# Strassen weight sums made in place, a weight ring of five, and a regrouped ConvFFN tail in a streaming encoder

## The reference

```python
h = rms_norm(x, norm1_g)
z = h @ w_in                       # 1024 x 4608: A value, A gate, B's B, C and v, merge gates
u = a_val * sigmoid(a_gate)
u = silu(layer_norm(causal_dwconv31(u) + b_dw_a))
y_a = u @ w_a_out
y_b = (b_g * causal_dwconv3(c_g * b_val)) @ w_b_out
x = x + (sigmoid(gA) * y_a + sigmoid(gB) * y_b) @ w_o
f_gate, f_val = split(rms_norm(x, norm2_g) @ w_up)       # 2 x 2816
x = x + (silu(causal_dwconv3(f_gate)) * f_val) @ w_down
y = rms_norm(x, final_g)
```

## Time and profile before

| | |
|---|---|
| Median of 3 runs | 1561.84 us (1561.3 to 1563.38) |
| Profiled execution | 1564.04 us, of which span 1561.1 us |
| PE, DVE, ACT, POOL busy | 90%, 71%, 34%, 5% of the span |
| Mean granted clock of PE | 0.969 of full |
| HBM read | 87.77 MB |

### The profile page before, as it was taken

One profiled execution on the slowest core, in us unless ns is written; L12 is line 12 of the kernel. 1 busy time (PEld: TensorE's weight loads), 2 busy tenths in 40 slices (PEclk: granted clock), 3 DMA queues, 4 the chain that ended last, 5 costly groups with the idle time before them and its releaser, 6 DMA issues.

```text
span 1561.1 us, 25790 instructions
## 1 busy us (share of the span) xinstructions
PE 1403.1 (90%) x10658; PEld 1369.0 (88%) x10658; DVE 1111.0 (71%) x1622; ACT 525.4 (34%) x854; POOL 79.5 (5%) x88
## 2 busy tenths in 40 slices
PE   4799999899996899997989999999999999999967
PEld 2699999898986899986889898999999898989967
DVE  5989999998865443467776667676667766676745
ACT  6743322333433333345422222323222222223122
POOL 2000000000000042211000000000000000000001
PEclk9999999999998899988899999999999999999988
DMA  5121111122214353321111111111121111111013
GB/s 167 49 74 48 48 55 48 63 83 98 99 65 147 112 180 106 89 61 48 55 47 42 48 35 55 41 42 55 31 64 35 48 41 48 35 55 35 27 41 116
DMA packets 137659, 102.98 MB, mean 66 GB/s; under 512 B 5389, under 2 KB 130055, under 8 KB 137543
## 3 DMA queue, kind: packets, MB, share of 16 engines
q1 hardware_dynamic: 134716, 92.21, 19.5%
q10 hardware_dynamic: 2827, 9.13, 1.5%
HBM read 87.77 MB, written 13.55 MB: 65 GB/s over the span
## 4 chain that ended last, share of the span: by engine, by line
PE 46%; DVE 28%; issue 10%; ACT 8%; DMA 6%; POOL 1%; ACTq 0%; SPq 0%; DVEq 0%
DVE cv L1297 6%; PE BA L369 5%; PE BC L369 5%; PE BA L371 5%; PE BA L370 5%; PE BC L371 5%; PE BC L370 5%; DMA w_raw<-in_w_down 4%; DVE cvf L1532 4%; DVE w_lo L1115 4%; ACT w_hi L749 3%; PE BB L369 3%; PE BB L370 3%; PE BB L371 3%; PE BS L369 2%
## 5 line engine op out<-in xcount | busy, mean ns | idle before, releaser
L1115 DVE TENSOR_TENSOR w_lo<-stg,w_hi 128x512 fp32r<-128x512 f32 x301 | 214.4, 714 | 130.5 <-ACT w_hi L749 129.6
L749 ACT ACTIVATE w_hi<-stg 128x512 fp32r<-128x512 f32 x301 | 187.9, 626 | 292.2 <-PE BA L371 91.3
L369 PE MATMUL BB<-hb,w_hi 128*128 128x272 f32 x788 | 233.1, 296 | 35.1 <-ACT ss_f L831 22.6
L369 PE MATMUL BA<-hb,w_hi 128*128 128x272 f32 x812 | 238.7, 294 | 23.9 <-DVE t_out L1195 8.1
L370 PE MATMUL BA<-hb,w_hi 128*128 128x272 f32 x812 | 235.7, 290 | 0.0
L371 PE MATMUL BA<-hb,w_lo 128*128 128x272 f32 x812 | 235.6, 290 | 0.0
L370 PE MATMUL BB<-hb,w_hi 128*128 128x272 f32 x788 | 229.7, 291 | 0.0
L371 PE MATMUL BB<-hb,w_lo 128*128 128x272 f32 x788 | 229.2, 291 | 0.0
L369 PE MATMUL BC<-hb,w_hi 128*128 128x272 f32 x640 | 187.3, 293 | 14.6 <-ACT ss_f L822 12.4
L1115 DVE TENSOR_TENSOR w_lo<-w_raw,w_hi 128x512 fp32r<-128x512 f32 x92 | 68.2, 741 | 167.6 <-ACT w_hi L749 167.0
L369 PEld LDWEIGHTS BB<-hb,w_hi 128*128 128x128 f32 x788 | 151.6, 192 | 40.7 <-ACT ss_f L831 25.0
(11 more groups left out here) (285 smaller groups left out, 3136.0 us busy)
## 6 DMA issues: line engine op xcount, KB each, us to landing
stg<-in_w_up SPq DMA_DIRECT2D x92, 256.0 KB, 3.0
stg<-in_w_in SPq DMA_DIRECT2D x80, 256.0 KB, 2.9
w_raw<-in_w_down SPq DMA_DIRECT2D x44, 256.0 KB, 2.7
gate_spill<-t_out ACTq DMA_DIRECT2D x16, 544.0 KB, 3.2
gates<-gate_spill SPq DMA_DIRECT2D x16, 544.0 KB, 4.5
w_raw<-in_w_o SPq DMA_DIRECT2D x32, 256.0 KB, 2.9
xr<-in_x_prompt SPq DMA_DIRECT2D x8, 512.0 KB, 5.8
out_y_prompt<-out_rows SPq DMA_DIRECT2D x8, 512.0 KB
```

Of the source, the lines that this page charges most:

```text
L369: pe.matmul(dst, w_hi[:, w, at:at + P], hi, start=first, stop=False, skip_group_check=True)
L749: act.activation(w_hi[:, n % RING, :], src, ACT.Copy).then_inc(whi, 1)
L1115: dve.tensor_tensor(out, full, high.bitcast(F32), ALU.subtract).then_inc(done, 1)
```

## The change

It has eight parts.

1. RING = 5 and LOOK = 4. `stg` shrinks from eight buffers to four.
2. The four sums are made in the place of their first terms: SP loads A22, A11, A12 and A21 into `stg[S1]`, `stg[S2]`, `stg[S4]`, `stg[S3]` (`first_terms`), and DVE adds in place (`weight_sums`), as a first step of `lo(n)` where product n + 1 has a sum as its weight. With LOOK = 4 that is in slots 3 (one sum), 4 (two) and 5 (one).
3. A11, A12 and A22 as weights of products 0, 5 and 6 are loaded a second time, by `plain_weights`, into the ring. A job has seven loads instead of four.
4. ConvFFN's `ss5` has two buffers, used by turns.
5. The groups of the last two pairs are ordered as job 41, job 42, `down(9)`, `down(10)`; the operands of f = 20 and 21 get places of their own (`qt_hi`, `qt_lo`, `qt_raw`).
6. `qb` is split in jobs 18 and 19 (blocks 0 and 1) and after job 19 (2 and 3). The adds for `e_b` move from POOL to DVE, slot 0 of job 19. The first mean part moves from behind product 1 to behind product 2, its copies to slots 4 and 6.
7. `ln_part` moves from h = 6, 7 to h = 7, 8, and both row copies stand in m = 4. In ConvFFN's first job `ms_columns(1)`, `root_diagonal(1)`, `rb_part(1)` and `rb_copy(1)` move back, the last two into the next job.
8. At the start, the rows of the second half of the tokens are normalised, turned and split later (`evac` in slots 4 to 11), job 0's sums are spread over its `lo` calls, and the fourth row tile is loaded ahead of the weights.

The table TAPS is the same in both kernels.

```diff
-RING = 4
-LOOK = 3
+RING = 5
+LOOK = 4
...
-    N_WD.append(BASE[-1] + 7)
+    BASE += [BASE[-1] + 7, BASE[-1] + 14]
+    N_WD += [BASE[-1] + 7, BASE[-1] + 11]
...
-    stg = place("stg", [P, 8, 4 * P], F32)
+    stg = place("stg", [P, 4, 4 * P], F32)
...
-    ss5_f = place("ss5_f", [P, 2, HP], F32, SS_AT + 8 * HP)
+    ss5_f = [place(f"ss5_f{s}", [P, 2, HP], F32, SS_AT + 8 * HP * (1 + s)) for s in range(2)]
...
-                    elif h in (6, 7):
-                        ln_part(h - 6)
+                    elif h in (7, 8):
+                        ln_part(h - 7)
...
-            job(J_F, [None, None, lambda: ms_columns(1), None, None, lambda: rb_part(1)])
-            job(J_F + 1)
+            job(J_F, [None, None, None, lambda: ms_columns(1)])
+            job(J_F + 1, [None, lambda: rb_part(1)])
...
+            job(f_job(KF - 2))
+            job(f_job(KF - 1))
+            down(G - 2)
...
+                    elif j > J_F + 2:
+                        act.wait_ge(n2, N2[j - 2])
                     act.activation(ss5(j), BC[:, ps, 0:HP], ACT.Copy).then_inc(cp, 1)
...
+            def qb_split_hi(k):
+                act.wait_ge(x_dve, X_DVE[J_S - 1])
+                if k == 1:
+                    act.wait_ge(wlo, BASE[J_F - 1] + 5)
+                elif k == 2:
+                    act.wait_ge(used, N_P1)
+                act.activation(qb_hi[k][:, :], bv[:, k, :], ACT.Copy).then_inc(qb_hid, 1)
...
+            def weight_sums(j, s):
+
+                terms = {S1: ((S1, S3),), S2: ((S3, S2), (S2, S1)), S4: ((S4, S2),), S3: ()}[s]
+                for a, b in terms:
+                    dve.wait_ge(base_in[a], 16 * (j + 1))
+                    dve.wait_ge(base_in[b], 16 * (j + 1))
+                    if a != S1:
+                        dve.wait_ge(wsum, 4 * j + SUM_NO[a] - 1)
+                    dve.tensor_tensor(stg[:, a, :], stg[:, a, :], stg[:, b, :], ALU.add).then_inc(wsum, 1)
+
             def lo(n):
+
+                if n + 1 in SUMMED:
+                    weight_sums(*SUMMED[n + 1])
...
+                    if j == J_F - 1 and s == 0:
+                        dve.wait_ge(tap_done, KA * TAPS_A)
+                        dve.tensor_tensor(e_b[:, :], cv[0][:, :], cv[1][:, :], ALU.add).then_inc(e_sum, 1)
...
+            def first_terms(j):
 
                 src = w_in_cols if j < J_F else w_up_cols
                 c1, c2 = job_cols(j)
+                for s, t, c, last in ((S1, 1, c2, 3), (S2, 0, c1, 4), (S4, 1, c1, 4), (S3, 0, c2, 5)):
+                    if j == J_F:
+                        sp.wait_ge(used, N_P2)
+                    elif j:
+                        sp.wait_ge(wlo, BASE[j - 1] + last)
+                    sp.dma_start(stg[:, s, :].rearrange("p (k c) -> p k c", k=KJ),
+                                 src[:, :, t, c:c + P]).then_inc(base_in[s], 16)
+
+            def job_weights(j):
...
                 if j:
+                    plain_weights(BASE[j], src[:, :, 0, c1:c1 + P])
+                if j + 1 < len(JOBS) and j + 1 != J_F:
+                    first_terms(j + 1)
+                plain_weights(BASE[j] + 5, src[:, :, 1, c1:c1 + P])
+                plain_weights(BASE[j] + 6, src[:, :, 1, c2:c2 + P])
```

More of the change, by code:

```diff
@@ L123, in streaming_encoder @@
     UP = at[0]
-    A11, A12, A21, S2, S3, S4, A22 = 0, 1, 2, 3, 4, 5, 6
-    S1 = A21
+    S1, S2, S4, S3 = range(4)
     T1N, T3, T2N, T4, B11, B21, B22 = range(7)
@@ L551, in _ @@
                             a = PW * p + HP * c
[L552 removed]
+                            last = three(bank[:, c, 0:HP], n % RING, k * P, qb_hi[k][:, a:a + HP], qb_lo[:, k, a:a + HP],
                                          k == 0, k == KB - 1)
@@ L634, in _ @@
             G = KF // 2
-            for i in range(1, G):
+            for i in range(1, G - 1):
                 job(f_job(2 * i))
@@ L733, in hi @@
                     act.wait_ge(used, n - RING + 1)
-                if n in DIRECT:
-                    act.wait_ge(w_in[n % RING], DIRECT[n])
+                if n in PLAIN:
+                    act.wait_ge(w_in[n % RING], PLAIN[n])
                     src = w_raw[:, n % RING, :]
                 else:
[L738 to L748, removed]
+                    j, s = SUMMED[n]
+                    act.wait_ge(wsum, 4 * j + SUM_NO[s])
+                    src = stg[:, s, :]
                 act.activation(w_hi[:, n % RING, :], src, ACT.Copy).then_inc(whi, 1)
@@ L952, in row_copy @@
                 act.activation(sq_a[:, lo:up], flat(BB)[:, 0:up - lo], ACT.Copy).then_inc(row_out, 1)
-            act.wait_ge(used, N_P1)
-            act.wait_ge(x_dve, X_DVE[J_S - 1])
-            for k in range(KB):
-                act.activation(qb_hi[:, k, :], bv[:, k, :], ACT.Copy).then_inc(qb_hid, 1)
+            qb_split_hi(2)
+            qb_split_hi(3)
             merge_sigmoid(J_F - 1, 1, 0)
@@ L1120, in lo @@
                 dve.wait_ge(whi, n + 1)
-                if n in DIRECT:
-                    src = w_raw[:, n % RING, :]
-                else:
-                    j = max(j for j in range(len(BASE)) if BASE[j] <= n)
-                    src = stg[:, (A11, S1, S2, S4, S3, A12, A22 + j % 2)[n - BASE[j]], :]
+                src = w_raw[:, n % RING, :] if n in PLAIN else stg[:, SUMMED[n][1], :]
                 sub(w_lo[:, n % RING, :], src, w_hi[:, n % RING, :], wlo)
@@ L1306, in _ @@
             lo(0)
-            for i in range(4):
-                weight_sum(0, i)
             blocks_b_lo(0)
@@ L1575, in ffn_slots @@
                             value(f, 0)
-                        elif s == 4:
+                        elif s == 4 and split:
                             ffn_lo(f)
```

302 lines of the change are left out of this document (153 added, 149 removed).

## The result

Forecast 1568 us (range 1545 to 1582), measured **1657.57 us** (median of four runs, 1650.69 to 1664.58) against 1562.39 (1561.3 to 1563.38) before. The ratio is 1.061, with a 95% interval of 1.0564 to 1.0655. The change makes the kernel slower, as forecast, but by 95 us instead of 6, and the time lies far outside the range. The profiled execution has a span of 1654.2 us (before: 1561.1).

The account below looks back on a forecast made before the run. PE was busy 90% of the span, with DVE setting the pace in jobs 5 to 18. The terms summed to +5.9 us on 1564.04, giving 1569.9; less 2.2 for the runs' median, the forecast was 1568 us, range 1545 to 1582.

Parts of the forecast that it names:

- The ring's price: Jobs 4 to 12: direct loads start only when PE frees the slot, A12 waits behind S3; +20.2 us.
- The signs I named: Jobs 5 to 11 over 23.5 us, 16 to 18 over 24.5, DVE idle 2 to 3 us before slot 1's `lo`.
- jobs 13 to 18: S jobs: late A12 load, slowed by gates sent to DRAM in the same slot; 2.8 us a job, +16.8 us.
- heavier traffic: Rival, chance 0.18: 129 more loads meet spills and each other; S jobs 3.7 us each, start +5, total 1578 us.
- `qb`, mean and LayerNorm steps: Around jobs 18 and 19 and after: `qb` and mean +1.6 us, LayerNorm chain sooner by 5.5 us.
- The start: DVE nearly always busy from 32 to 79 us, its work only reordered; 0 us (-5 to +5).
- half jobs: Jobs 2 and 3, products of 1.5 us: half of the ring's delay, 2.1 us a job, +4.2 us.
- The end: `down(9)` between job 42 and the last group covers PE's 14.3 us wait; -18.2 us.
- The pairs: ConvFFN: two buffers end the L822 wait, L831 stays at 1.6, sums delay the fifth add; -10.3 us.
- POOL's adds: Jobs 12 and 15: moving the adds off POOL ends a 2.4 us DVE hold-up in each; -4.3 us.
- The ring's delay finds cover: Rival, chance 0.27: in slot 1 of jobs 5 to 18 A12 isn't held behind S3; 1541 us, half of it 1554.
- All three cases: Rivals: ring's delay covered (0.27), heavier traffic (0.18), and cancelling, ring losing about 32 us instead of 37, 1559 to 1565 (0.15).

Follow-up runs that it names:

- Experiment 4: Changed kernel with the gates' two 544 KB transfers to DRAM issued in slot 4 of the next job, not slot 1; 1640.68 us.
- Experiment 2: Changed kernel with each gate load of the `w_b_out` and `w_a_out` stages issued behind the next block's plain load, not ahead of it; 1628.64 us.
- experiment 10: Changed kernel with ring 4 and look-ahead 3, as before the change, all else as changed; 1629.59 us.
- experiment 11: The fastest kernel (1481.61 us) with the three adds into `e_b` back on POOL; 1486.96 us.
- experiments 1 to 7 and 9: Changed kernel with look-ahead 3, reordered loads or later gate transfers, singly or combined; from 1640.68 to 1481.61 us.
- experiment 3: Changed kernel with A12's load into the ring issued ahead of the first term of S3 in SP's queue; 1631.24 us.
- e5_look3_order: Changed kernel with look-ahead 3, ring still 5, and A12's load ahead of the first term of S3; 1525.17 us.
- e6_look3_order_spill: Changed kernel with look-ahead 3, A12's load ahead of the first term of S3, and the gates' transfers issued in slot 4; 1504.98 us.
- e12_traffic: Kernel before the change with 129 more 256 KB loads, copied to spare DRAM, that no engine waits for; 1602.49 us.

## Why the prediction was wrong

**The ring's price, right in kind.** The steps "A12 is issued about 0.7 us behind the end of `lo` in slot 0" and "its `hi` can start some 3.4 us after that end" hold where nothing collides: in job 9 of the changed kernel `lo` ends at 249.23, the `hi` starts at 253.30, 4.1 us later, and DVE waits 3.75 us ahead of `lo` in slot 1. The signs I named came: jobs 5 to 11 took 23.5 to 27.5 us, `hi` is released by `w_raw` from `in_w_in`. Jobs 4 to 12 cost 26.9 instead of 17.8. The term that was too small is the lateness in slot 1: against the start of its job `lo` of slot 1 came 28.7 us later than before, summed over these nine jobs, where I had 21.6. The landing was about 0.7 us longer. A22 did not add to it: in slot 2 of these jobs DVE waits for nothing. The rows of job 9, DVE and then ACT:

```profile
248.55 0.68 DVE L1133 TENSOR_TENSOR w_lo<-stg,w_hi 128x512 fp32r<-128x512 f32 x1
...
253.97 0.69 DVE L1133 TENSOR_TENSOR w_lo<-w_raw,w_hi 128x512 fp32r<-128x512 f32 x1 [3.75 <-ACT w_hi L752]
```

```profile
253.30 0.63 ACT L752 ACTIVATE w_hi<-w_raw 128x512 fp32r<-128x512 f32 x1 [3.45 <-DMA w_raw<-in_w_in]
```

That the queue behind S3 was half of it was overrated: taking it away alone gave 0.7 a job, until the loads also had a product's time of room.

**Step that failed first: jobs 13 to 18, "I take 2.8 a job".** The slot was found, the collision with the spill too, but priced by bandwidth ("256 KB take 0.8 us; two blocks among the spill get 1 to 2 us more"). Measured was 5.5 us a job, net. The load is not slowed a little among the gates, it comes after them: 6.2 us from issue to Copy. Experiment 4 takes 16.9 us back by moving nothing but the issue of the gates. The rival "heavier traffic" had this mechanism at a third of its size: 0.9 us a job over the forecast, where 2.7 were measured.

**Step that failed most: no term at all for `w_b_out` and `w_a_out`.** I reasoned that "RING and LOOK both grow by one, so the load starts as late relative to its slot as before", and that holds. But LOOK also sets what stands ahead of what on DVE, and `gate_row` a place in SP's queue at a fixed distance of 4. At 3 the wait for piece i-4 was long over when SP came to it; at 4 it is the newest merge. This is +37.3 where I had -5.2. Experiment 2 shows 28.9 of it, experiment 10 that look-ahead 3 takes away 39. What remains there at ring 4 and look-ahead 3 (`e10_ring4`), 271.6 against 273.2, is the net of the `qb`, mean and LayerNorm steps: -1.6 where I had -5.2 with 1.0 for the ring. In that kernel the wait for `qb_lo` fell from 9.9 to 3.7 us and LayerNorm's from 4.7 to 1.8 (3.2 and 4.2 in the changed kernel), so `qb` gave more than forecast (6.2 for 2.5) and LayerNorm less (2.9 for 5.5); waits that are new there (3.5 us of issue on PE, 1.6 for the copy of the mean) took most of it back, and these I haven't followed.

**The start: "DVE is nearly always busy [...] 0".** Busy it had been, but the plain blocks now stand in its order as well: DVE's waits for `w_hi` between 28 and 92 us rose from 4.2 to 13.1 us, which is 8.9 of the +10.4. `lo` of the first direct block waits 5.8 us at 49.97, another 3.2 at 69.44, and PE's turns of x stand behind the same `hi` on ACT. The **half jobs** failed alike: I halved the delay because the products are half as long, but a load takes no less time for that: `lo` of slot 1 came 5.1 and 5.2 us later, and the jobs cost +5.4 each instead of +2.1. The start and the half jobs rest on these rows; no run was made for either alone.

**What held.** The end: -17.2 for -18.2. The pairs: -11.7 for -10.3, as a sum of parts of which the buffer was worth more (some 2 us a pair) and the adds behind the sums cost 0.9 (+0.85 forecast; PE's waits for `stream` between 840 and 1470 us rose from 3.5 to 11.5). So the total is nearer than its parts, which is luck. L831 was to stay at 1.6; its successor L836 shows 15.0 us in nine, 1.7. POOL's adds: 5.4 measured in experiment 11, 4.3 forecast. The sentence on the Trainium skill (DMA: Bandwidth & Descriptors, section Rules for kernel authors: issue early, compute, wait late) turned out the best guide: the kernels of experiments 1 to 7 and 9 make the same loads and differ in look-ahead, in when the loads are issued and in what is sent ahead of them, and their times run from 1641 down to 1482 us.

**The rivals.** "The ring's delay finds cover" needed A12 not to be held behind S3; even so (experiment 3) the kernel became only 26 us faster than the changed one and stayed 4% slower than the kernel before. "Heavier traffic" pointed the right way. All three cases and the range took the ring's cost for a matter of the jobs; none had a closed loop between two queues.

**Not settled.** Why look-ahead 4 costs 5 to 10 us over ring 4 and look-ahead 3 between job 19 and job 20 even with the gates reordered (276.5 to 281.5 against 271.6); by the rows at 672.71 to 673.56 the loads of residual rows stand in the same place as the gates did, but that order wasn't tried. The matmuls at the lower clock are up to 29.4 us of the +93.1, by PE's busy time; they came with the waits, and no run separated the two.

## What to carry to other kernels

When a look-ahead or a ring grows, two numbers change: the room (ring less look-ahead), which sets how early a load can start at the earliest, and the look-ahead itself, which shifts one engine's order against every queue that waits at a fixed distance; go round each circle of engine, queue and buffer with the new numbers before you price anything. A load issued when its slot comes free paid here all of its latency and the transfers just sent ahead of it, so price it with the neighbour's whole transfer, not with a share of bandwidth. And what looks like a loss of the idea can be one of its order: the same blocks in the same ring, with one block less of look-ahead and issued first, made this the fastest version.

## What the runs showed of the hardware

- A load of 256 KB issued within 1.1 us of two transfers of 544 KB was ready for its Copy after 6.2 us in job 17 of the changed kernel and after 6.9 in that of `e5_look3_order`. With the gates moved to slot 4 it was ready after 3.6 us in `e4_spill` and 4.3 in `e6_look3_order_spill`, and in the ConvFFN job of the earlier trace rows, where it was issued at 941.46, after 2.7.
- 129 loads more, in job 17 with a DMA share of 0.41 for 0.28, left jobs 3 to 18 at their length to the tenth of a microsecond, where every load had time in hand (`e12_traffic`).
- A DVE instruction that began 0.44 us after a 2.99 us add on POOL took 3.15 us instead of 0.86, here a `TENSOR_SCALAR` (`e11_pool`); in the earlier trace rows it was a subtraction that took 3.10 instead of 0.69.
- Waits cost more than their length: the same 10658 matmuls kept PE busy for 1403.1 us before, 1432.5 in the changed kernel (granted clock 0.81 and 0.89 in the stages that wait in each block) and 1378.1 in the fastest.
